# A second tile that projects only its 1024 new columns, row tiles transposed by DMA, and another start order

## The reference

```python
h = jnp.concatenate([meta, x], axis=1)
u = rms_norm(h, g_mix[l])
z = u @ w_in[l]                        # value | gate | pool | gate A | gate B, 1024 each
gates = jax.nn.sigmoid(z[..., c3:] + b_gate[l])
y_conv = conformer_conv(z[..., :c1], z[..., c1:c2], ...)   # GLU, depthwise conv of width 31, LN, silu, matmul
y_pool = multi_scale_pool(z[..., c2:c3], ...)  # centred window means of 2, 4, 8, 16 minus the token, two matmuls
merged = gates[..., :D_MODEL] * y_conv + gates[..., D_MODEL:] * y_pool
h = h + merged @ w_o[l]
v = rms_norm(h, g_ffn[l])
f = jax.nn.silu(v @ w_ffn_gate[l]) * (v @ w_ffn_up[l])     # 2816 wide
h = h + f @ w_ffn_down[l]
h = rms_norm(h, g_final)
```

## Time and profile before

| | us |
|---|---|
| median of 3 runs | 1039.08 (1039.0 to 1039.71) |
| the profiled execution | 1040.15 |
| its span, slowest core (core 0) | 1038.6 |
| spans of the 8 cores | 1034.1 to 1038.6 |
| PE busy in the span | 1010.3 (97%) |
| DVE, ACT, GpSimd busy | 429.4, 296.3, 176.6 |

### The profile page before, as it was taken

One profiled execution on the slowest core, in us unless ns is written; L12 is line 12 of the kernel. 1 busy time (PEld: TensorE's weight loads), 2 busy tenths in 40 slices (PEclk: granted clock), 3 DMA queues, 4 the chain that ended last, 5 costly groups with the idle time before them and its releaser, 6 DMA issues.

```text
span 1038.6 us, 16871 instructions; the slowest of 8 cores (1034.1 to 1038.6 us)
## 1 busy us (share of the span) xinstructions
PE 1010.3 (97%) x5900; PEld 498.3 (48%) x5900; DVE 429.4 (41%) x630; ACT 296.3 (29%) x521; POOL 176.6 (17%) x329
## 2 busy tenths in 40 slices
PE   6879999999999999999999999999999999999996
PEld 2545555444454444444456555544445444444442
DVE  4445545742472233221345565574247121211133
ACT  4324455512152222211113334551215211111111
POOL 2411122011122112210231111101112211111010
PEclk9999999999999999999999999999999999999999
DMA  9998795363339968640939879335332955554022
GB/s 227 154 246 176 145 208 81 77 97 55 68 124 170 153 114 132 95 74 1 172 98 249 190 145 172 53 79 93 61 64 79 153 73 80 80 74 71 1 72 101
DMA packets 68148, 118.37 MB, mean 114 GB/s; under 512 B 18465, under 2 KB 18465, under 8 KB 68066
## 3 DMA queue, kind: packets, MB, share of 16 engines
q0 software_dynamic: 38592, 70.27, 44.1%
q1 hardware_dynamic: 27170, 38.90, 13.8%
q10 hardware_dynamic: 2304, 8.13, 2.0%
HBM read 159.72 MB, written 8.39 MB: 162 GB/s over the span
## 4 chain that ended last, share of the span: by engine, by line
PE 93%; DMA 3%; SPq 2%; issue 1%; DVE 1%; ACT 0%; DVEq 0%; POOL 0%; POOLq 0%; ACTq 0%
PE ps L378 87%; PE ps L511 5%; SPq L214 2%; DMA wr<-wst 1%; DMA rep<-aT 1%; PE ps L410 1%; DMA h<-xe 1%; DVE ub L400 0%; DVEq L922 0%; ACT sqj L388 0%; POOL stats L391 0%; ACT uT L421 0%; ACT sqj L732 0%; DVE h L730 0%; DVE aT L481 0%
## 5 line engine op out<-in xcount | busy, mean ns | idle before, releaser
L378 PE MATMUL ps<-vT,wr 128*128 128x512 bf16 x1408 | 304.9, 379 | 0.0
L378 PE MATMUL ps<-uT,wr 128*128 128x352 bf16 (+2 forms) x1664 | 292.9, 335 | 4.8 <-DMA wr<-wst 4.2
L214 POOL DMA_DIRECT2D wr<-wst x268 | 143.4, 538 | 695.5 <-PE ps L378 638.3
L378 PEld LDWEIGHTS ps<-uT,wr 128*128 128x128 bf16 x1664 | 161.9, 98 | 132.2 <-issue 15.9
L378 PEld LDWEIGHTS ps<-vT,wr 128*128 128x128 bf16 x1408 | 137.5, 98 | 164.7
L378 PE MATMUL ps<-wr,fT 128*128 128x512 bf16 x704 | 152.3, 379 | 0.0
L712 DVE TENSOR_TENSOR fT<-ps,sgf 128x512 bf16<-128x512 f32 x88 | 60.8, 691 | 217.2 <-PE ps L378 191.8
L711 ACT ACTIVATE sgf<-ps 128x512 f32<-128x512 f32 x88 | 52.5, 597 | 227.9 <-PE ps L378 227.9
L378 PEld LDWEIGHTS ps<-wr,fT 128*128 128x128 bf16 x704 | 68.9, 98 | 83.1
L511 PE MATMUL ps<-rep,wr 128*32 128x512 bf16 x1024 | 59.9, 388 | 6.5 <-DMA rep<-aT 5.7
L732 ACT ACTIVATE sqj<-h 128x512 bf16<-128x512 f32 x32 | 20.1, 630 | 134.0 <-DVE h L730 134.0
(11 more groups left out here) (70 smaller groups left out, 639.2 us busy)
## 6 DMA issues: line engine op xcount, KB each, us to landing
wr<-wst POOLq DMA_DIRECT2D x268, 256.0 KB, 6.4
rep<-aT SPq DMA_DIRECT2D x256, 65.8 KB, 5.8
xt<-xe SPq DMA_DIRECT2D x24, 512.0 KB, 4.4
out<-h ACTq DMA_DIRECT2D x15, 512.0 KB, 2.6
h<-xe SPq DMA_DIRECT2D x8, 512.0 KB, 8.7
wpt<-wpt SPq DMA_DIRECT2D x4, 256.0 KB, 9.8
gb_s<-gb SPq DMA_DIRECT2D x2, 512.0 KB, 9.2
xt<-xe SPq DMA_DIRECT2D x2, 128.0 KB, 5.7
```

The lines of the kernel that those rows point to most:

```text
L214: e.dma_start(out=o[1], in_=o[2]).then_inc(o[3], 16)
L378: S.op(PE, lambda e: e.matmul(out, lhsT=lhsT, rhs=rhs, start=start, stop=stop), [lhsT, rhs], [out], signal=signal)
```

## The change

- `EXT` becomes 1056, and the first tile's column blocks are 352, 352 and 352. The second tile's are two of 512 at columns 32 and 544 (`TCOLS`). Its columns 0 to 31 are copied on DVE: in `uT` at the start of the FFN of the first tile, in the conv input per chunk (`cA`, saved in `im2col` of the first tile, put back ahead of the second tile's DMAs), in the pool input per chunk (`cP`, in `poolcols`). The second tile then has 8 row tiles in place of 9.
- In the W_o stage of both tiles, row tiles 0 to 5 are transposed by DMA from SP's queue (`v_transpose`), each issued one step earlier than the PE transpose stood; row tiles 6 and 7 stay on PE. Each transposing DMA has a semaphore of its own.
- `START` is written anew: fewer zero matmuls, one weight load (val1) after the fifth row tile's statistics and one (gate1) after the sixth, where both stood after the second and third; chunk 0's matmuls on block 1 ahead of chunk 1's on block 0; the third block of chunk 0 ahead of chunk 1's second; evictions mostly on DVE. The broadcast of the first gain row (`gb`) is now behind two zero matmuls, with the first row tile's statistics between its two copies.
- In `rel`, while `lead` is 8, GpSimd waits for PE to have finished what stands ahead in program order before it issues the loads.
- `stats` has 6 slots for 12 and `hsum` is packed, to make room for `cA` and `cP`.

```diff
--- before.py
+++ after.py
@@ -22,10 +22,10 @@
 NT = TOK // TT
 NB = TT // 512
 HALO = 15
-EXT = TT + 2 * HALO + 1
+EXT = TT + 2 * HALO + 2
 REPW = EXT - 3
 EXTP = 1056
-XROWS = TOK + 2 * HALO + 2
+XROWS = TOK + EXT - TT
 WINS = (2, 4, 8, 16)
 RMS_EPS = 1e-6
 LN_EPS = 1e-5
@@ -42,8 +42,8 @@
 P2_STEPS = ["G0", "G1", "P0", "P1", "G2", "P2", "G3", "Y0.0", "Y1.0", "Y2.0", "Y0.1", "Y1.1", "Y2.1", "P3", "Y3.0", "Y3.1"]
 for _c in range(4, KC):
     P2_STEPS += [f"G{_c}", f"P{_c}", f"Y{_c}.0", f"Y{_c}.1"]
-START = """L3 I4 A0 B0 T0 I4 L4 A1 E0d W1 B1 T1 I4 L5 A2 E1d W1 B2 T2 A3 E2d B3 G00 T3 L6 A4 E3a W1 B4 H00 T4 L7 A5 E4d W1 B5
-V00 G10 T5 C0 A6 E5a W1 B6 H10 G01 T6 A7 E6d W1 B7 V10 H01 T7 A8 E7a V01 B8 G11 H11 T8 W2 E8d G02 H02 V11 V02 R0
+START = """L3 B0 T0 I4 L4 A1 E0d B1 T1 I4 L5 A2 E1d B2 T2 L6 A3 B3 E2d T3 A4 W1 G00 E3d L7 A5 W1 B4 T4 H00 A6 E4a B5 T5
+V00 C0 A7 W1 E5d G01 B6 T6 H01 A8 W1 E6a B7 T7 V01 G10 E7d B8 T8 W2 H10 E8d G02 H02 V10 G11 H11 V02 R0 V11
 G12 H12 V12 S0""".split()
 
 
@@ -255,10 +255,12 @@
     ident = fix.get("ident_s", [128, 128], BF16)
     ones = fix.get("ones_s", [128, 128], F32)
     nhalf = fix.get("nhalf_s", [128, 16], F32)
-    hsum = fix.get("hsum", [128, 8, 16], F32)
+    hsum = fix.get("hsum", [128, 16], F32)
+    cA = fix.get("cA", [128, KC, 32], BF16)
+    cP = fix.get("cP", [128, KC, 32], F32)
     lnst = fix.get("lnst", [128, 32], F32)
     invc = fix.get("invc_s", [128, 32], F32)
-    NST = 12
+    NST = 6
     stats = fix.get("stats", [128, NST, 16], F32)
     tmp8 = fix.get("tmp8", [128, 16], F32)
     R0 = fix.cur
@@ -325,7 +327,7 @@
     POOL = Rec("pool", sem("s_pool"))
     SP = Rec("sp", sem("s_sp"))
     gb_sem = [Prod(sem(f"d_gb{i}"), 16) for i in range(3)]
-    tr_sem = [Prod(sem(f"d_tr{i}"), 16) for i in range(2)]
+    tr_sem = [Prod(sem(f"d_tr{i}"), 16) for i in range(17)]
     wpt_sem = [Prod(sem(f"d_wpt{i}"), 16) for i in range(2)]
     cst = [Prod(sem(f"d_cst{i}"), 16) for i in range(3)]
     ring_sem = [Prod(sem(f"d_wr{i}"), 16) for i in range(RING)]
@@ -363,6 +365,8 @@
 
     def rel(k=1):
         wstate["freed"] += k
+        if wstate["lead"] < RING:
+            S._waits(POOL, {PE: PE.count})
         room = wstate["li"] + wstate["lead"] - wstate["next"]
         if room > 0:
             prefetch(min(room, k + 1))
@@ -429,38 +433,40 @@
     def norm_transpose(n, dstT, col0, q, eng=None):
         transpose_evict(n, dstT, col0, transpose_mm(n, q), eng)
 
-    SUBS = [(r, min(128, EXT - r)) for r in range(0, EXT, 128)]
+    TSUBS = [[(r, min(128, EXT - r)) for r in range(0, EXT, 128)], [(32 + r, 128) for r in range(0, TT, 128)]]
+    SUBS = TSUBS[0]
     xbuf = {}
 
     def s0_load(i, idx):
-        r, n = SUBS[idx]
+        r, n = TSUBS[i][idx]
         row0 = i * TT + r
         if i == 0 and idx < 8:
             buf, sm = h1[idx], xh_sem[idx]
         else:
             buf, sm = xt[idx % 3], xt_sem[idx % 3]
         xbuf[(i, idx)] = buf
-        n = (n + 15) // 16 * 16
         S.dma(SP, sm, buf[0:n, :], xe.ap()[row0:row0 + n, :])
 
     def s0_chain(i, idx):
-        r, n = SUBS[idx]
-        n = (n + 15) // 16 * 16
+        r, n = TSUBS[i][idx]
         norm_chain(xbuf[(i, idx)][0:n, :], n, 0, idx % NUB)
 
     def s0_transpose(i, idx):
-        r, n = SUBS[idx]
-        n = (n + 15) // 16 * 16
-        xbar_transpose(SP, tr_sem[idx % 2], uT[:, :, r:r + n], ub[idx % NUB][0:n, :])
-
-    COLS = [(0, 352), (352, 352), (704, 351)]
+        r, n = TSUBS[i][idx]
+        xbar_transpose(SP, tr_sem[idx], uT[:, :, r:r + n], ub[idx % NUB][0:n, :])
+
+    TCOLS = [[(0, 352), (352, 352), (704, 352)], [(32, 512), (544, 512)]]
+    ct = [0]
+
+    def carry(o, i_):
+        S.op(DVE, lambda e: e.tensor_copy(out=o, in_=i_), [i_], [o])
 
     vg_w = {}
 
     def half_mm(c, bi, w):
         if c not in vg_w:
             vg_w[c] = (take(f"val{c}"), take(f"gate{c}"))
-        c0, n = COLS[bi]
+        c0, n = TCOLS[ct[0]][bi]
         bk = nb()
         mm8(bk, vg_w[c][w], lambda k: uT[:, k, c0:c0 + n], n)
         return bk
@@ -485,6 +491,11 @@
         vg_evict(c, bi, vg_mm(c, bi))
 
     def im2col(c):
+        at = aT[c % 3]
+        if ct[0] == 0:
+            carry(cA[:, c, :], at[:, TT:EXT])
+        else:
+            carry(at[:, 0:EXT - TT], cA[:, c, :])
         st = c % 3
         tot = rep_sem[st].count + 16 * 16
         for s_ in range(4):
@@ -527,11 +538,15 @@
 
     def poolcols(i, c):
         wp = take(f"pool{c}")
-        for (c0, n) in COLS:
+        for (c0, n) in TCOLS[i]:
             bp = nb()
             mm8(bp, wp, lambda k: uT[:, k, c0:c0 + n], n)
             po, pi_ = psb[:, c0:c0 + n], psum[bp][:, 0:n]
             S.op(ACT, lambda e, po=po, pi_=pi_: e.activation(out=po, in_=pi_, func=AF.Copy), [pi_], [po])
+        if i == 0:
+            carry(cP[:, c, :], psb[:, TT:EXT])
+        else:
+            carry(psb[:, 0:EXT - TT], cP[:, c, :])
         rel(1)
         g = c // 2
         w = WINS[g]
@@ -695,6 +710,9 @@
         if s + 3 < 8:
             xres_load(i, s + 3)
 
+    def v_transpose(s):
+        xbar_transpose(SP, tr_sem[9 + s], vT[:, :, s * 128:(s + 1) * 128], ub[s % NUB][:])
+
     ff_w = {}
     fi = [0]
 
@@ -754,7 +772,7 @@
         for st in steps:
             k = int(st[1:])
             if st[0] == "v":
-                for bi in range(3):
+                for bi in range(len(TCOLS[i])):
                     vg_block(k, bi)
                 vg_done(k)
             elif st[0] == "p":
@@ -787,12 +805,6 @@
         for j in range(k):
             mm(psum[b_][:], zt[:, 0:128], zt[:], True, True, j == k - 1)
 
-    idle_mm(4)
-    for h in range(2):
-        b_ = nb()
-        g_i, g_p, g_o = grow[:, h * 512:(h + 1) * 512], psum[b_][:], gb[:, 0, h * 512:(h + 1) * 512]
-        mm(g_p, ones[0:1, :], g_i, True, True, True)
-        S.op(DVE, lambda e, g_o=g_o, g_p=g_p: e.tensor_copy(out=g_o, in_=g_p), [g_p], [g_o])
     rs0 = {}
 
     def row_a(k):
@@ -811,6 +823,19 @@
     def row_e(k, eng):
         r, n = SUBS[k]
         transpose_evict(n, uT, r, tb[k], eng)
+
+    idle_mm(2)
+    gbp = []
+    for h in range(2):
+        b_ = nb()
+        g_i, g_p = grow[:, h * 512:(h + 1) * 512], psum[b_][:]
+        mm(g_p, ones[0:1, :], g_i, True, True, True)
+        gbp.append(g_p)
+    for h in range(2):
+        g_p, g_o = gbp[h], gb[:, 0, h * 512:(h + 1) * 512]
+        S.op(DVE, lambda e, g_o=g_o, g_p=g_p: e.tensor_copy(out=g_o, in_=g_p), [g_p], [g_o])
+        if h == 0:
+            row_a(0)
 
     vb = {}
     for st in START:
@@ -845,6 +870,7 @@
             {"A": row_a, "B": row_b, "T": row_t}[st[0]](k)
 
     for i in range(NT):
+        ct[0] = i
         if i == 0:
             rel(2)
             im2col(1)
@@ -886,8 +912,8 @@
             if s >= 1:
                 norm_scale(h1[s - 1][:], 128, 1, (s - 1) % NUB, prs)
             prs = rms_rstd(h1[s][:], 128)
-            if s >= 2:
-                norm_transpose(128, vT, (s - 2) * 128, (s - 2) % NUB)
+            if 1 <= s <= 6:
+                v_transpose(s - 1)
         norm_scale(h1[7][:], 128, 1, 7 % NUB, prs)
         rel(8)
         ffn(0, 0)
@@ -900,6 +926,7 @@
         ffn(2, 1)
         nxt = i + 1 < NT
         if nxt:
+            carry(uT[:, :, 0:EXT - TT], uT[:, :, TT:EXT])
             s0_load(i + 1, 0)
             s0_load(i + 1, 1)
             s0_load(i + 1, 2)
@@ -908,11 +935,11 @@
             ffn(f, 0)
             ffn(f, 1)
             idx = (f - 3) // 2
-            if nxt and f % 2 == 0 and idx < 9:
-                if idx + 1 < 9:
+            if nxt and f % 2 == 0 and idx < 8:
+                if idx + 1 < 8:
                     s0_chain(i + 1, idx + 1)
                 s0_transpose(i + 1, idx)
-                if idx + 3 < 9:
+                if idx + 3 < 8:
                     s0_load(i + 1, idx + 3)
         down(i, 0)
         down(i, 1)
```

More of the change, by code:

```diff
@@ L730, in down @@
             S.op(DVE, lambda e, ho=ho, pdi=pdi: e.tensor_tensor(out=ho, in0=pdi, in1=ho, op=ALU.add), [pdi, ho], [ho])
-            sh = hsum[:, s, h:h + 1]
+            sh = hsum[:, 2 * s + h:2 * s + h + 1]
             S.op(ACT, lambda e, ho=ho, sh=sh: e.activation(out=sqj[:, 0:512], in_=ho, func=AF.Square, scale=1.0 / 32.0,
@@ L736, in down @@
                 me, rs = st[:, 0:1], st[:, 1:2]
-                s0_, s1_ = hsum[:, s, 0:1], hsum[:, s, 1:2]
+                s0_, s1_ = hsum[:, 2 * s:2 * s + 1], hsum[:, 2 * s + 1:2 * s + 2]
                 S.op(DVE, lambda e, me=me, s0_=s0_, s1_=s1_: e.scalar_tensor_tensor(
```

## The result

The changed kernel takes 1026.46 us (median of four executions; 1025.32 to 1026.95), the kernel before 1039.08 in the same series (median of 1039.0, 1039.08 and 1039.71); the ratio is 0.9875, 95% interval 0.9856 to 0.9895. In some executions of any of these kernels some of the cores are slowed to a lower clock (a fourth one of the kernel before took 1247.19); such executions are left out everywhere. The profiled execution has a span of 1025.4 us, 13.2 less than before. The forecast was 1023.7, with a range of 1018 to 1031.

A forecast was written before the change was run, and what follows sets the result against it. PE's instruction stream was taken to bound 950 us, and arrivals the first 80. Savings of 5.4 (transposes), 1.6 (second tile) and 8.4 (start), together 15.4 us, came off 1039.08, giving 1023.7; range 1018 to 1031.

The forecast's parts named there:

- Part 2, the transposes: W_o stage of both tiles: twelve transpose groups of 0.45 us leave PE, worth 5.4 us in full.
- Cost: none: W_o stage: the DMA transposes make nobody wait, since row tile 3 has 8.1 us to land and needs 3.8.
- The third rival: W_o stage: DMA transposes queue up, 7.9 us of waiting per tile at 6.6 us each, 1039.5 or slower; 4 in 100.
- Part 1, the second tile: Second tile's projections: 16 wide matmuls per unit for 24 narrow save 2.7 us, of which 1.6 arrive.
- the 1.1 us that I took off for SP's queue: Second tile's last convolution: its wait for copies issued by SP grows by 1.1 us, cutting 2.7 to 1.6.
- Part 3, the start: Start of the kernel: four terms, 1.6 + 1.8 + 3.3 + 1.7, save 8.4 us, with bounds of 3 and 12.
- (a): End of START: earlier row tiles bring it from 43.7 to 42.1 us, 1.6 sooner; bounds 3.6 sooner to 2 later.
- (b): First convolution: its copies are issued from 38.3 us instead of 42.17, so its wait goes, saving 1.8 us.
- (c): Second convolution: with fewer weight loads queued, its 3.90 us wait for copies falls to 0.6, saving 3.3.
- (d): Second convolution: without the gap before it, it stays at full clock, saving 1.7 us.
- the signs of the start that were named in advance: Copy waits at most 1 us before 80 us, at most four queued loads, clock 1.00 from 40, second convolution at 67 to 68.
- the first rival: Start gives back little: two half-clock stretches, START no sooner, half the waits left; worth 3 us, total 1029.1; 24 in 100.

## Why the prediction was right, and where it was not

**Part 2, the transposes: right.** 5.4 us predicted, 2 x 2.7 measured by stage, 5.8 by time. The landing was taken from the earlier trace rows, 3.8 us, and came out at 3.9 (3.1 to 4.8) on core 7; row tile 3 was down 2.5 to 4.7 us before the FFN, as 8.1 - 3.8 = 4.3 says. By an estimate from the page of the Trainium skill that speaks against it ("VectorE: DVE Perf Modes", "The three transpose paths") eight blocks would take 10.5 us; the trace disagrees, 3.1 to 5.7 over the cores and tiles. But "Cost: none" was right by less than it seemed: I asked whether a transpose lands in time by itself, and not what would be ahead of it. The third rival priced a queue of transposes (6.6 us each); what makes them late is a burst of weight loads, which costs 12 us at once. Row tiles 6 and 7 were left on PE in this kernel, and for row tile 7 that is worth 26 us as long as the loads are not held.

**Part 1, the second tile: right in kind, too small.** 2.7 us for the matmuls was 3.0, since the wide ones run at 216 ns also on `uT`, and not 216.7. The step that failed is the 1.1 us that I took off for SP's queue. It rested on the earlier trace rows, the waits of one core; the table by stage shows that the other seven cores had none in the same execution. After the change all eight have 1.4 to 2.8 us to spare at the last convolution, counted from the last copy's landing. Of the sum's own core the part gave 4.1 us where 1.6 were predicted, since the wait of 1.1 us that was to grow went away. Why core 0's issues were slow in that execution (83.9 us for 128 of them, the other cores 77.2 to 83.1, all cores after 74.6 to 78.3) I have not tested.

**Part 3, the start: the direction right, the size not.** 8.4 us predicted; 5.9 in the median of the cores, 3.7 from slowest to slowest core. By its terms:

- (a) `START` 1.6 us sooner: failed. The last row tile's transpose came at 34.0 us in the median of the cores (36.4 before), where I had 32.9, and seven blocks follow it where four did; by my own count 34.5 (43.7 - 9.2) is where the two meet. Taken as the start of the first convolution less its wait and 96 matmuls, `START` ended at 42.7 for 43.1 before, 0.4 sooner (42.0 where the changed kernel was profiled again). The experiment with the old order shows no difference in the time. I also counted no half-clock stretch. In the mean of the cores there were 4.7 us of them from the first full-clock stretch to 58 us, before 3.0, and 10.2 on the slowest core.
- (b) the first convolution's wait, 1.8 us: half right. It went from 1.5 to 0.3 us in the median, but is up to 2.1. The bound that I took for the copies, 6 us, was exceeded: 6.7 to 10.4, since GpSimd, let go when `START` ends, issued four loads into the middle of them.
- (c) and (d), the second convolution, 3.3 and 1.7 us: right. Its wait went from 3.9 to 0.4 in the median, the half-clock stretches behind 58 us from 4.3 us per core to 0.4. From the first convolution's start to the third's, the mean of the cores fell by 5.0 us, which is what the two terms add up to. The experiment without GpSimd's wait brings back 3.2 of these.

So the signs of the start that were named in advance came out in part. The second convolution starts at 67.8 to 68.1 us on three cores, but at 69.3 in the median and 72.7 at the latest; PE waits more than 1 us for the copies on four cores; and on one the clock dips at 61.5, behind such a wait.

**The slowest core, and luck.** The sum was made on core 0, the slowest before. It gained 18.1 us, more than predicted. But another core is the slowest after, since the start differs by 5 us from core to core, and the forecast had no term for that. From the slowest core before to the slowest after, the start gave 3.7 us for the 8.4 predicted, close to the 3 of the first rival; the second tile gave 4.1 for 1.6; the transposes 5.4 for 5.4. These come to 13.2 for 15.4: the time lies near the forecast by luck as well, since the forecast had 4.7 us too much for the start and 2.5 us too little for the second tile, and the two errors half cancel.

## What to carry to other kernels

A DMA that PE will soon wait for can have a price that is set by what else is in the DMA engines, and not by its own size (here 15 us in place of 3, with eight loads issued in the 1.6 us before it and just after): look for the moment at which a prefetcher is let go, and put a wait or an earlier load there. Read a wait on all cores before it becomes a term of the sum; if only one core of eight has it, it is not the kernel's. And where the time is that of the slowest core, the part of the kernel that differs between cores is to be forecast by its worst core, not by that of the profile. And compare the traces stage by stage to the very end before a gain is put down to the edit: more than half of what the copies on GpSimd's queue gave came behind the last matmul.

## What the runs showed of the hardware

- A DMA transpose of a 128x1024 bf16 row tile lands in 3.0 to 3.1 us where no other load stands near it, in 3.4 to 5.7 beside the residual loads of the changed kernel, in 13.3 to 17.2 when it is issued just behind the first of eight loads of 256 KB; it holds SP's queue for 1.22 us, a plain load of a row tile for 0.33.
- The copies of 66 KB land in 2.0 us in empty engines; on the slowest core, in 6.4 to 10.5 once four weight loads are under way.
- GpSimd's closing instruction took 7.37 us, and 6.38 in the versions that issue 16 copies from its queue; the span ends with it.
- On all eight cores at once, with PE busy for 98% of the span, the granted clock was 1.00 in every stage behind the start of the changed kernel.
